# A state space layer on one core: the quarter turns move from TensorE to ScalarE, and TensorE multiplies constants ahead of some waits

## The chip, the cores and the metric

The kernel runs on one core of one Trainium2 chip. Its engines work in parallel and are ordered by semaphores: TensorE (PE, with its weight loads PEld), VectorE (DVE), ScalarE (ACT), GpSimd (POOL) and SyncE (SP), whose queue issues most transfers. The metric is the device time of one launch in microseconds, the median of the runs.

## The reference, cut to what matters

The whole is a stack of layers over 512 tokens of width 1024: an S5 layer, gated feed-forward layers, an attention layer, and then a second block (a Mamba-2 layer and a differential attention layer). The change touches the first layer alone:

```python
def s5_mixer(xn, w_in, lam_re, lam_im, b_re, b_im, c_re, c_im, d_skip, log_dt, w_glu):
    u = (xn @ w_in)                       # 512 x 1024, 64 groups of 16 inputs
    a_bar = exp(lam * dt)                 # complex, 64 states for each group
    b_bar = ((a_bar - 1.0) / lam)[..., None] * b_mat
    s = recurrence(s = a_bar * s + b_bar @ u_t)   # along the sequence
    y = real(s @ c) + d_skip * u
    val, gate = split(gelu(y) @ w_glu)
    return val * sigmoid(gate)
```

The states are complex. The kernel keeps the 64 real parts of a group in partitions 0 to 63 and the 64 imaginary parts in partitions 64 to 127. It takes 8 tokens as one step, so that 64 steps remain, and removes the phase: it multiplies the input of step c by the phase exp(-i c t), runs a real recurrence with the decay alone (one scan instruction), and turns the result back by exp(i c t). A complex product of that kind needs the vector itself and the vector turned by a quarter, (re, im) to (-im, re), which exchanges the two halves of the partitions and changes one sign.

## The kernel before, in words

The S5 layer lies at about 10 to 205 us of the span. Its 64 groups are taken in eight octets, q = 0 to 7. One list, S5_ORDER (s5_order, L90), is walked by every engine's own program (s5_pe, s5_act, s5_dve, s5_pool, s5_sp); each engine does its part of a step and skips the steps in which it has none, strictly in the order of the list. In the loop over q the steps are, in order: `drive q+1`, `scan q`, `inB q+2`, `state q`, then at q = 2 and 3 half of the last input product, `turnB q+2`, `swap q+1`, `inC q+2`, `read q`, `near q+2`, and at some q post steps (the skip term, GELU and the splitting of the result for the next product).

What each does for an octet:

- `inB` and `inC` (combine, L2087): VectorE builds the tables Bp and CA out of powers of a_bar and B or C, three large elementwise instructions each.
- `turnB`: TensorE transposes Bp into PSUM banks 2 and 3 (L2114), ScalarE copies them out to BT (L2122).
- `near`: TensorE makes the short range kernel out of Bp and CA (bank 4, L2132), ScalarE copies it out (ksb, L2143), SP's queue stores it and loads it back as a table Mt.
- `drive`: TensorE multiplies BT by the inputs U (bank 6, L2177). ScalarE makes the sines and cosines s and c of the octet (L2211, L2212, L2215), copies the product out to V (L2218), and starts the angles of the next octet: eight small copies with a scale (angles_act, L2194).
- `swap`: TensorE multiplies V by the constant matrix mturn, a quarter turn (bank 7, L2245).
- `scan`: VectorE forms turned V times s (L2253), V times c (L2256), their sum (L2258), and runs the recurrence (L2263), which writes Ss.
- `state`: TensorE multiplies Ss by the constant matrix turn (bank 0, L2269). VectorE multiplies that by s into H (L2281) and Ss by c in place (L2283; from q = 5, APART, a third instruction adds both, L2285 and L2287). ScalarE makes the decays of the next octet (rho_act, L2225).
- `read`: TensorE waits for H, then multiplies Mt by U and CA by H and by Ss (bank 1; L2297, L2299, L2300, from q = 5 L2297 and L2302). ScalarE copies the result out (Y, L2310), SP's queue stores it.

The scan of q waits until read q-1 is over, since that reads Ss. The weights of the input products are split in two parts by ScalarE (L390) and VectorE (L401) shortly ahead of their product. After the loop the gated output product follows, and then the rest of the network.

Of the kernel before, what the change touches and what calls it, by code (L numbers as in the profile page):

```python
# [8 lines left out]
P = 128  # L9
T = 512  # L10
# [6 lines left out]
NC = 64  # L17
# [24 lines left out]
for _name, _w in PARAMS:  # L42
# [3 lines left out]

CONSTS = [("ones", 128), ("sel", 32), ("spread", 128), ("ident", 128), ("ntri", 128), ("nones", 128),
          ("upper", 128), ("slower", 128), ("nupper", 128), ("low", 128), ("alibi", 512)]
S5_CONSTS = [("turn", 128), ("mturn", 128), ("count", 64)]
CCOL = {}  # L50
_n = 0
for _name, _w in CONSTS:
# [25 lines left out]


def s5_constants():  # L80
    turn = np.zeros((P, P))
    turn[np.arange(64) + 64, np.arange(64)] = -1.0
    turn[np.arange(64), np.arange(64) + 64] = 1.0
    count = np.broadcast_to(np.arange(64.0)[None, :], (P, 64))
    return np.concatenate([turn, -turn, count], axis=1).astype(np.float32)

# [9 lines left out]
def s5_order():  # L98


    posts = {3: "0a 1a", 4: "2a 3a"}
    out = [("dense", 0), ("use", 0), ("dense", 1), ("use", 1), ("load", 0), ("prep", 4),
           ("dense", 2), ("use", 2),
           ("load", 1), ("prep", 5), ("dense", 3), ("use", 3), ("prep", 6), ("dense", 4), ("inB", 0), ("turnB", 0),
           ("use", 4), ("dense", 5), ("prep", 7), ("drive", 0), ("inC", 0), ("near", 0), ("loadbc", 3), ("inB", 1),
           ("use", 5), ("turnB", 1), ("swap", 0), ("inC", 1), ("dense", 6), ("near", 1)]
    for q in range(8):
        if q < 4:
            out.append(("loadbc", q + 4))
        if q < 6:  # L110
            out.append(("load", q + 2))
        if q < 7:
            out.append(("drive", q + 1))
        if q == 6:
            out.append(("splithigh", 0))
        out.append(("scan", q))
        if q < 6:
            out.append(("inB", q + 2))
        if q == 0:
            out.append(("use", 6))  # L120
        if q == 6:
# [12 lines left out]
        if q < 6:
            out.append(("turnB", q + 2))
        if q < 7:
            out.append(("swap", q + 1))
        if q == 4:
            out += [("postb", 0), ("postb", 1)]
        if q < 6:  # L140
            out.append(("inC", q + 2))
        if q == 3:
            out.append(("use", 7))
        if q == 7:
            out.append(("glu", 0))
# [1819 lines left out]
W = NQ  # L1965
# [2 lines left out]
GS = [slice(q * W, (q + 1) * W) for q in range(8)]  # L1968
LOW, UP = slice(0, 64), slice(64, 128)
APART = 5  # L1970


def flat(x):
# [130 lines left out]
    dve.e.tensor_tensor(by_lag(dst, n), by_lag(dst, n), by_lag(K.Bs, n), ALU.add).then_inc(K.S["mat"], 1)  # L2104


def turn_b_pe(K, pe, q):
    pe.wait_ge("mat", 2 * q + 1)
    pe.wait_ge("ld", 16)
    pe.wait_ge("ld5", 16)  # L2110
    for j in range(2):
        take(pe, 2 + j, ("BT", 2 * q + j + 1))
        for i in range(4):
            mm = pe.e.transpose(K.bank[2 + j][:, i * P:(i + 1) * P], K.Bp[:, 4 * j + i, :], K.con("ident"))  # L2114
        mm.then_inc(K.S["BTp"], 1)
# [9 lines left out]

def near_pe(K, pe, q):

    pe.wait_ge("mat", 2 * q + 2)
    take(pe, 4, ("ksb", 2 * q + 2))
    for g in range(8):  # L2130
        j, i = g // 4, g % 4
        mm = pe.e.matmul(K.bank[4][32 * j:32 * j + 16, i * P:(i + 1) * P], K.Bp[:, g, 0:16], K.CA[q % 3][:, g, 0:P],  # L2132
                         start=(i == 0), stop=True, skip_group_check=True)
    mm.then_inc(K.S["Kp"], 1)
# [35 lines left out]


def drive_pe(K, pe, q):
    take(pe, 6, ("V", q + 1))
    pe.wait_ge("BT", 2 * q + 2)
    pe.wait_ge(f"ul{q % 3}", 128 * (q // 3 + 1))
    for i in range(8):
        mm = pe.e.matmul(K.bank[6][:, i * NC:(i + 1) * NC], K.BT[q % 2][:, i, :], K.U[q % 3][:, i, :], start=(i == 0),  # L2177
                         stop=True, skip_group_check=True)
    mm.then_inc(K.S["Vp"], 1)

# [26 lines left out]
def drive_act(K, act, q):  # L2207
    c, s = K.rot[q % 2][:, 0], K.rot[q % 2][:, 1]
    act.wait_ge("trig", q + 1)
    act.other("sin")  # L2210
    act.e.activation(s, K.rsc[:, :, :], ACT.Sin, scale=-6.283185).then_inc(K.S["rot"], 1)  # L2211
    act.e.activation(c, K.rsc[:, :, :], ACT.Abs, scale=6.283185).then_inc(K.S["rot"], 1)  # L2212
    act.wait_ge("rot", 4 * q + 2)
    act.wait_ge("prep", 2)
    act.e.activation(c, c, ACT.Sin, scale=-1.0, bias=K.quarter[:, :]).then_inc(K.S["rot"], 1)  # L2215
    act.wait_ge("Vp", q + 1)
    act.wait_ge("vr", q - 1)
    act.e.activation(flat(K.V[q % 2]), K.bank[6][:, :], ACT.Copy).then_inc(K.S["V"], 1)  # L2218


def rho_act(K, act, q):
# [17 lines left out]
                               op1=ALU.subtract).then_inc(K.S["trig"], 1)  # L2239


def swap_pe(K, pe, q):
    take(pe, 7, ("vr0", q + 1))
    pe.wait_ge("V", q + 1)
    pe.e.matmul(K.bank[7][:, :], K.five("mturn"), flat(K.V[q % 2]), start=True, stop=True).then_inc(K.S["turned"], 1)  # L2245


def scan_dve(K, dve, q):
    c, s, V, e = K.rot[q % 2][:, 0], K.rot[q % 2][:, 1], K.V[q % 2], dve.e
    dve.wait_ge("turned", 2 * q + 1)  # L2250
    dve.wait_ge("rot", 4 * q + 1)
    dve.wait_ge("S", q)
    e.tensor_tensor(K.vr[:, :, :], K.bank[7][:, :].rearrange("p (g c) -> p g c", g=W), s, ALU.mult).then_inc(  # L2253
        K.S["vr0"], 1)
    dve.wait_ge("rot", 4 * q + 3)
    own(K, dve, "dve", e.tensor_tensor(V[:, :, :], V[:, :, :], c, ALU.mult))  # L2256
    dve.wait_ge("vr0", q + 1)
    e.tensor_tensor(K.vr[:, :, :], K.vr[:, :, :], V[:, :, :], ALU.add).then_inc(K.S["vr"], 1)  # L2258
    dve.wait_ge("rot", 4 * q + 4)
    dve.wait_ge("vr", q + 1)  # L2260
    dve.wait_ge("H", q)
    dve.wait_ge("Yp", min(q, APART))
    e.tensor_tensor_scan(flat(K.Ss), flat(K.rho), flat(K.vr), 0.0, ALU.mult, ALU.add).then_inc(K.S["S"], 1)  # L2263


def state_pe(K, pe, q):
    take(pe, 0, ("H0", q + 1))
    pe.wait_ge("S", q + 1)
    pe.e.matmul(K.bank[0][:, :], K.five("turn"), flat(K.Ss), start=True, stop=True).then_inc(K.S["turned"], 1)  # L2269


def state_dve(K, dve, q):


    c, s, S, H, e, n = K.rot[q % 2][:, 0], K.rot[q % 2][:, 1], K.Ss, K.H, dve.e, NC - 1
    b = K.bank[0][:, :].rearrange("p (g c) -> p g c", g=W)
    dve.wait_ge("Yp", q)
    if q == APART:
        e.memset(H[:, :, 0:1], 0.0).then_inc(K.S["dve"], dve.up())
    dve.wait_ge("turned", 2 * q + 2)  # L2280
    e.tensor_tensor(H[:, :, 1:NC], b[:, :, 0:n], s[:, :, 0:n], ALU.mult).then_inc(K.S["H0"], 1)  # L2281
    if q < APART:
        e.tensor_tensor(S[:, :, 0:n], S[:, :, 0:n], c[:, :, 0:n], ALU.mult).then_inc(K.S["H"], 1)  # L2283
        return
    own(K, dve, "dve", e.tensor_tensor(S[:, :, 0:n], S[:, :, 0:n], c[:, :, 0:n], ALU.mult))  # L2285
    dve.wait_ge("H0", q + 1)
    e.tensor_tensor(H[:, :, 1:NC], H[:, :, 1:NC], S[:, :, 0:n], ALU.add).then_inc(K.S["H"], 1)  # L2287


def read_pe(K, pe, q):  # L2290
    take(pe, 1, ("Y", q + 1))
    pe.wait_ge("H0", q + 1)
    pe.wait_ge("H", q + 1)
    pe.wait_ge(f"mt{q % 2}", 128 * (q // 2 + 1))
# [103 lines left out]
def s5_pe(K, pe):  # L2398
# [6 lines left out]
    for what, q in S5_ORDER:  # L2405
# [3 lines left out]
            product_half(K, pe, "a_w_in", 7, FIRST[7], x, ("us", 8), q)  # L2409
        elif what == "drive":  # L2410
            drive_pe(K, pe, q)
        elif what == "swap":
            swap_pe(K, pe, q)
        elif what == "state":
            state_pe(K, pe, q)
        elif what == "read":
            read_pe(K, pe, q)
        elif what == "turnB":
# [21 lines left out]
def s5_act(K, act):  # L2440
# [13 lines left out]
    for what, q in S5_ORDER:  # L2454
# [6 lines left out]
        elif what == "drive":  # L2461
# [2 lines left out]
                rho_act(K, act, 0)  # L2464
            if q < 7:
                angles_act(K, act, q + 1)
        elif what == "state" and q < 7:
            rho_act(K, act, q + 1)
        elif what == "read":
            read_act(K, act, q)  # L2470
        elif what == "turnB":
# [714 lines left out]
```

## Time and profile before

| what | value |
|---|---|
| median of 3 runs | 2039.47 us (2038.74 to 2039.65) |
| profiled execution, its own time | 2048.49 us |
| its span | 2046.7 us |
| PE busy | 1969.8 us, 96% |
| DVE busy | 1380.8 us, 67% |
| ACT busy | 865.7 us, 42% |
| granted TensorE clock, mean | 0.987 |

The span is the time from the first to the last instruction of the profiled execution, and that execution took some 9 us longer than the median of the runs. The granted clock is a share of TensorE's full speed: 1.00 is 2.4 GHz, 0.50 is 1.2 GHz.

### The profile page before, as it was taken

What the parts mean: (1) busy time and instruction counts of PE and PEld (TensorE: products, weight loads), DVE (VectorE), ACT (ScalarE), POOL (GpSimd) and SP (SyncE); (2) the same over time, 40 slices, a digit from 0 to 9 for tenths busy, and PEclk for the clock granted to TensorE, in tenths of its full rate; (3) what the DMA queues carried; (4) which work ended last, traced back from release to release, by engine and by line L of the source; (5) the groups of instructions that cost most, each with busy time, mean ns of one, the idle gap of its engine ahead of it and who ended that gap; (6) DMA issues with size and microseconds to landing.
All of it is one profiled execution on the core that took longest, in us unless ns stands there. A gap on an engine that the chain in (4) does not pass through costs nothing.

```text
span 2046.7 us, 24942 instructions
## 1 busy us (share of the span) xinstructions
PE 1969.8 (96%) x9404; PEld 1566.5 (77%) x9404; DVE 1380.8 (67%) x2046; ACT 865.7 (42%) x1342; POOL 254.1 (12%) x231
## 2 busy tenths in 40 slices
PE   7899999999999999999999999899999998999997
PEld 5687888888888776788888888687777776886665
DVE  7986467536654448747645654888888888437986
ACT  4554343222233338733222233444444444236773
POOL 3030100000001000010000001224333331000002
PEclk9898999999999999999999999999999999999998
DMA  7454323232233220022233323221222223322112
GB/s 224 107 126 129 114 82 105 80 123 85 89 95 106 91 92 21 1 93 92 82 105 104 103 79 100 73 67 53 83 73 83 78 63 93 103 73 74 35 32 78
DMA packets 79623, 178.33 MB, mean 87 GB/s; under 512 B 17680, under 2 KB 31248, under 8 KB 79504
## 3 DMA queue, kind: packets, MB, share of 16 engines
q1 hardware_dynamic: 75792, 169.92, 26.8%
q0 software_dynamic: 3424, 6.23, 1.3%
q8 instruction: 75, 1.23, 0.2%
q10 hardware_dynamic: 288, 0.59, 0.1%
q14 instruction: 44, 0.36, 0.1%
HBM read 169.43 MB, written 7.27 MB: 86 GB/s over the span
## 4 chain that ended last, share of the span: by engine, by line
PE 71%; DVE 18%; ACT 5%; issue 5%; DMA 0%; POOL 0%; DVEq 0%; POOLq 0%; ACTq 0%
PE psum L430 16%; PE psum L433 16%; PE psum L431 16%; DVE wl L401 2%; PE psum L471 2%; PE psum L472 2%; PE psum L474 2%; PE psum L855 1%; PE psum L856 1%; PE psum L857 1%; ACT wh L390 1%; PE psum L452 1%; DVE mE L1654 1%; PE psum L455 1%; DVE mE L1673 1%
## 5 line engine op out<-in xcount | busy, mean ns | idle before, releaser
L401 DVE TENSOR_TENSOR wl<-raw,wh 128x1024 fp32r<-128x1024 f32 (+3 forms) x337 | 391.7, 1164 | 330.8 <-ACT wh L390 330.3
L430 PE MATMUL psum<-xh,wh 128*128 128x512 f32 x1368 | 542.6, 397 | 1.2 <-DVE mbc L1531 0.9
L433 PE MATMUL psum<-xh,wl 128*128 128x512 f32 x1368 | 534.0, 390 | 1.3 <-DVE wl L401 1.3
L431 PE MATMUL psum<-xl,wh 128*128 128x512 f32 x1368 | 533.5, 390 | 0.0
L390 ACT ACTIVATE wh<-raw 128x1024 fp32r<-128x1024 f32 (+3 forms) x337 | 315.4, 938 | 275.3 <-PE psum L433 167.7
L430 PEld LDWEIGHTS psum<-xh,wh 128*128 128x128 f32 x1368 | 257.4, 188 | 62.2 <-issue 3.4
L433 PEld LDWEIGHTS psum<-xh,wl 128*128 128x128 f32 x1368 | 257.3, 188 | 57.2 <-DVE wl L401 2.9
L431 PEld LDWEIGHTS psum<-xl,wh 128*128 128x128 f32 x1368 | 257.5, 188 | 55.4 <-issue 2.9
L578 POOL TENSOR_TENSOR rs<-rs,sq 128x512 f32<-128x512 f32 x41 | 54.3, 1323 | 1092.3 <-ACT sq L563 1092.2
L430 PE MATMUL psum<-fh,wh 128*128 128x512 f32 x352 | 136.9, 389 | 0.0
L431 PE MATMUL psum<-fl,wh 128*128 128x512 f32 x352 | 136.9, 389 | 0.0
L433 PE MATMUL psum<-fh,wl 128*128 128x512 f32 x352 | 136.9, 389 | 0.0
L675 DVE TENSOR_TENSOR h<-h,psum 128x512 f32<-128x512 f32 x88 | 60.1, 683 | 70.0 <-PE psum L433 67.6
L471 PE MATMUL psum<-xh,wh 128*128 128x512 f32 x160 | 67.1, 420 | 13.1 <-ACT wh L390 10.8
L431 PEld LDWEIGHTS psum<-fl,wh 128*128 128x128 f32 x352 | 66.1, 188 | 13.8
L433 PEld LDWEIGHTS psum<-fh,wl 128*128 128x128 f32 x352 | 66.1, 188 | 13.8
L430 PEld LDWEIGHTS psum<-fh,wh 128*128 128x128 f32 x352 | 66.1, 188 | 13.7
L541 ACT ACTIVATE xh<-h,par 128x512 fp32r<-128x512 f32 x64 | 44.1, 716 | 64.0 <-DVE h L675 55.3
L1663 ACT ACTIVATE mE<-psum 128x384 f32<-128x384 f32 x32 | 15.7, 491 | 117.2 <-DVE mE L1654 117.2
L474 PE MATMUL psum<-xh,wl 128*128 128x512 f32 x160 | 63.2, 395 | 0.0
L472 PE MATMUL psum<-xl,wh 128*128 128x512 f32 x160 | 63.1, 395 | 0.0
L727 ACT ACTIVATE ny<-ny 128x512 f32<-128x512 f32 x22 | 13.9, 632 | 110.3 <-DVE ny L764 110.3
(498 smaller groups left out, 3362.5 us busy)
## 6 DMA issues: line engine op xcount, KB each, us to landing
raw<-d_w SPq DMA_DIRECT2D x224, 512.0 KB, 3.5
raw<-d_w SPq DMA_DIRECT2D x32, 384.0 KB, 3.1
raw<-d_w SPq DMA_DIRECT2D x48, 256.0 KB, 2.6
raw<-d_w SPq DMA_DIRECT2D x32, 320.0 KB, 2.9
Mt<-d_kd SPq DMA_DIRECT2D x64, 64.0 KB, 2.4
bc<-d_bc SPq DMA_DIRECT2D x8, 256.0 KB, 3.4
d_ud<-ust SPq DMA_DIRECT2D x8, 256.0 KB, 3.1
U<-d_ud POOLq DMA_DIRECT2D x64, 32.0 KB, 3.0
```

The source lines that it names most:

```text
L390: act.e.activation(K.wh[n % NH][:, 0:COLS[n]], K.raw[n % RAW][:, 0:COLS[n]], ACT.Copy).then_inc(K.S["hi"], 1)
L401: dve.e.tensor_tensor(K.wl[n % NH][:, 0:COLS[n]], K.raw[n % RAW][:, 0:COLS[n]], K.wh[n % NH][:, 0:COLS[n]].bitcast(F32), ALU.subtract).the ...
L430: pe.e.matmul(b[:, :], WH[:, o:o + P], XH, start=(k == k0), stop=False)
L431: pe.e.matmul(b[:, :], WH[:, o:o + P], XL, start=False, stop=False)
L433: mm = pe.e.matmul(b[:, :], WL[:, o:o + P], XH, start=False, stop=(k == k1 - 1))
L452: pe.e.matmul(b[:, :], WH[:, o:o + P], XH, start=(k == 0), stop=False)
L471: pe.e.matmul(b[:, :], WH[:, o:o + P], XH, start=(k == 0), stop=False)
L472: pe.e.matmul(b[:, :], WH[:, o:o + P], XL, start=False, stop=False)
L474: mm = pe.e.matmul(b[:, :], WL[:, o:o + P], XH, start=False, stop=(k == 7))
L541: act.e.activation(K.xh[:, k, :], K.h[:, k, :], ACT.Copy, scale=K.par(gain, k)).then_inc(K.S["xh"], 1)
L578: pool.e.tensor_tensor(K.acc[:, :], K.acc[:, :], K.sq[k % 2][:, :], ALU.add).then_inc(K.S["acc"], 1)
L675: dve.e.tensor_tensor(K.h[:, m, :], K.h[:, m, :], K.bank[bank][:, :], ALU.add).then_inc(K.S[signal], 1)
```

## The change

The two constant matrices go, and with them the steps `swap` and the TensorE part of `state`. ScalarE makes the quarter turn instead, as two copies of 64 partitions each, the lower half into the upper and the upper into the lower, one of them with the scale -1: once out of the drive's PSUM bank in place of the copy to V (so V now holds the turned vector), once out of Ss into V (state_act). VectorE reads the vector that isn't turned straight from the drive's bank, which alternates between 6 and 7. TensorE gets 23 matmuls of the identity by 512 columns of constants, whose result nobody reads; they are issued ahead of the wait of turnB, near or read of the octets that the three tuples name.

```diff
-S5_CONSTS = [("turn", 128), ("mturn", 128), ("count", 64)]
+S5_CONSTS = [("count", 64)]
@@ s5_order: the steps ("swap", q) are gone
+BUSY_TURN = (5, 3, 3, 3, 0, 0, 3, 2)
+BUSY_NEAR = (0, 0, 2, 0, 0, 0, 0, 0)
+BUSY_READ = (0, 0, 0, 0, 0, 0, 1, 1)
+def busy_pe(K, pe, bank, n):
+    first = CCOL["spread"][0]
+    for _ in range(n):
+        pe.e.matmul(K.bank[bank][:, :], K.con("ident"), K.all_con[:, first:first + T], start=True, stop=True)
 def turn_b_pe(K, pe, q):
-    pe.wait_ge("mat", 2 * q + 1)
     ...
         take(pe, 2 + j, ("BT", 2 * q + j + 1))
+        if j == 0:
+            busy_pe(K, pe, 2, BUSY_TURN[q])
+            pe.wait_ge("mat", 2 * q + 1)
 def near_pe(K, pe, q):
+    take(pe, 4, ("ksb", 2 * q + 2))
+    busy_pe(K, pe, 4, BUSY_NEAR[q])
     pe.wait_ge("mat", 2 * q + 2)
-    take(pe, 4, ("ksb", 2 * q + 2))
 def drive_pe(K, pe, q):
-    take(pe, 6, ("V", q + 1))
+    bank = 6 + q % 2
+    take(pe, bank, ("vr0", 2 * q + 1))
 def drive_act(K, act, q):
     ...
-    act.wait_ge("vr", q - 1)
-    act.e.activation(flat(K.V[q % 2]), K.bank[6][:, :], ACT.Copy).then_inc(K.S["V"], 1)
+    act.wait_ge("H0", q - 1)
+    V, b = flat(K.V[q % 2]), K.bank[6 + q % 2]
+    act.e.activation(V[LOW, :], b[UP, :], ACT.Copy).then_inc(K.S["V"], 1)
+    act.e.activation(V[UP, :], b[LOW, :], ACT.Copy, scale=-1.0).then_inc(K.S["V"], 1)
+def state_act(K, act, q):
+    act.wait_ge("S", q + 1)
+    S, turned = flat(K.Ss), flat(K.V[q % 2])
+    act.e.activation(turned[LOW, :], S[UP, :], ACT.Copy, scale=-1.0).then_inc(K.S["turned"], 1)
+    act.e.activation(turned[UP, :], S[LOW, :], ACT.Copy).then_inc(K.S["turned"], 1)
-def swap_pe(K, pe, q): ...
-def state_pe(K, pe, q): ...
 def scan_dve(K, dve, q):
-    dve.wait_ge("turned", 2 * q + 1)
+    dve.wait_ge("Vp", q + 1)
+    dve.wait_ge("rot", 4 * q + 3)
     dve.wait_ge("S", q)
     # first product: the drive's bank times c, then V (turned) times s, then the sum
 def state_dve(K, dve, q):
     dve.wait_ge("turned", 2 * q + 2)
-    e.tensor_tensor(H[:, :, 1:NC], b[:, :, 0:n], s[:, :, 0:n], ALU.mult).then_inc(K.S["H0"], 1)
+    e.tensor_tensor(H[:, :, 1:NC], K.V[q % 2][:, :, 0:n], s[:, :, 0:n], ALU.mult).then_inc(K.S["H0"], 1)
 def read_pe(K, pe, q):
     take(pe, 1, ("Y", q + 1))
+    busy_pe(K, pe, 1, BUSY_READ[q])
 def s5_act(K, act):
         elif what == "drive":
             drive_act(K, act, q)
             ...
             if q < 7:
                 angles_act(K, act, q + 1)
-        elif what == "state" and q < 7:
-            rho_act(K, act, q + 1)
+        elif what == "state":
+            state_act(K, act, q)
+            if q < 7:
+                rho_act(K, act, q + 1)
```

## Rows read from the trace of the kernel before

**Rows 1.** Stages with each engine's busy time, granted clock (PEclk), DMA share.
```profile
93.60:97.40 3.80, 1.42 (x10) 1.13 (x10) 3.77 (x6) 3.38 (x12) 0.00 (x0) 1.00 0.37 80
97.40:111.00 13.60, 13.60 (x65) 12.14 (x64) 8.30 (x9) 1.75 (x4) 1.59 (x4) 0.50 0.18 43
...
169.10:172.50 3.40, 2.53 (x23) 2.56 (x23) 3.28 (x5) 0.19 (x1) 0.00 (x0) 1.00 0.52 137
172.50:189.50 17.00, 16.35 (x58) 13.66 (x58) 8.47 (x13) 7.19 (x11) 2.67 (x5) 0.50 0.51 148
```

**Rows 2.** PE's waits, 40 to 190 us: total, times, longest.
```profile
PE psum L2114 <- DVE Bp L2104: 11.4, 5, 4.4
```

**Rows 3.** VectorE in order of time, octets 3 and 4: start, length.
```profile
138.20 1.22 DVE L2263 TENSOR_TENSOR_SCAN xs<-rho,sq 128x512 f32<-128x512 f32 x1 [0.74 <-PE psum L2300]
142.85 0.68 DVE L2281 TENSOR_TENSOR H<-psum,rot 128x504 f32<-128x504 f32 x1
...
145.36 1.35 DVE L2096 TENSOR_TENSOR Bs<-pw,bc 128x1152 f32<-128x1152 f32 x1
149.29 0.69 DVE L2238 SCALAR_TENSOR_TENSOR sq<-rot,sq 128x512 f32<-128x512 f32 x1
151.99 1.23 DVE L2263 TENSOR_TENSOR_SCAN xs<-rho,sq 128x512 f32<-128x512 f32 x1
```

**Rows 4.** ScalarE in order of time, the same turn of the loop.
```profile
139.59 1.20 ACT L2143 ACTIVATE ksb<-psum 16x512 f32<-16x512 f32 x2 [0.89 <-PE psum L2132]
...
142.61 0.60 ACT L2218 ACTIVATE V<-psum 128x512 f32<-128x512 f32 x1
143.11 2.01 ACT L2194 ACTIVATE sq<-five,tau 128x64 f32<-128x64 f32 x8
145.02 0.61 ACT L2225 ACTIVATE rho<-s5small 128x504 f32<-128x504 f32 x1
```

**Rows 5.** TensorE in order of time, the same turn and the read ahead.
```profile
132.60 0.33 PE L2297 MATMUL psum<-U,Mt 128*128 128x64 f32 x2
...
138.00 1.50 PE L2132 MATMUL psum<-CA,Bp 128*16 128x128 f32 x16
139.43 2.00 PE L2177 MATMUL psum<-U,BT 128*128 128x64 f32 x16
...
142.99 1.09 PE L2114 MATMUL psum<-con,Bp 128*128 128x128 f32 x8 [0.66 <-DVE Bp L2104]
143.93 1.02 PE L2245 MATMUL psum<-V,five 128*128 128x512 f32 x2
144.79 0.33 PE L2297 MATMUL psum<-U,Mt 128*128 128x64 f32 x2
```

**Rows 6.** TensorE in order of time, octet 1, where the clock falls.
```profile
96.17 1.09 PE L2114 MATMUL psum<-con,Bp 128*128 128x128 f32 x8 [2.38 <-DVE Bp L2104]
97.10 1.62 PE L2245 MATMUL psum<-V,five 128*128 128x512 f32 x2
98.51 0.53 PE L2297 MATMUL psum<-U,Mt 128*128 128x64 f32 x2
...
108.78 2.56 PE L2132 MATMUL psum<-CA,Bp 128*16 128x128 f32 x16
```

**Rows 7.** VectorE, first and last product into H (octets 0 and 7).
```profile
79.95 0.67 DVE L2281 TENSOR_TENSOR H<-psum,rot 128x504 f32<-128x504 f32 x1
...
176.66 0.68 DVE L2281 TENSOR_TENSOR H<-psum,rot 128x504 f32<-128x504 f32 x1 [2.43 <-PE psum L2269]
```

**Rows 8.** ScalarE and TensorE near the loop's end, and ScalarE's first instruction.
```profile
175.39 1.28 ACT L2351 ACT_TABLE_LOAD   x1
178.53 0.63 ACT L2354 ACTIVATE xh<-py 128x512 fp32r<-128x512 f32 x1
185.72 0.77 PE L2385 MATMUL psum<-xl,wh 128*128 128x512 f32 x1
5.50 1.28 ACT L2993 ACT_TABLE_LOAD   x1 [5.50 <-DMA five<-d_five]
```

More of the change, by code:

```diff
@@ L80, in s5_constants @@
 def s5_constants():
[L81 to L85, printed above, removed]
+    return np.broadcast_to(np.arange(64.0)[None, :], (P, 64)).astype(np.float32)
 def pieces(k0, k1):
@@ L105, in s5_order @@
            ("use", 4), ("dense", 5), ("prep", 7), ("drive", 0), ("inC", 0), ("near", 0), ("loadbc", 3), ("inB", 1),
-           ("use", 5), ("turnB", 1), ("swap", 0), ("inC", 1), ("dense", 6), ("near", 1)]
+           ("use", 5), ("turnB", 1), ("inC", 1), ("dense", 6), ("near", 1)]
     for q in range(8):
@@ L135, in s5_order @@
             out.append(("turnB", q + 2))
-        if q < 7:
-            out.append(("swap", q + 1))
         if q == 4:
@@ L2176, in drive_pe @@
     for i in range(8):
-        mm = pe.e.matmul(K.bank[6][:, i * NC:(i + 1) * NC], K.BT[q % 2][:, i, :], K.U[q % 3][:, i, :], start=(i == 0),
+        mm = pe.e.matmul(K.bank[bank][:, i * NC:(i + 1) * NC], K.BT[q % 2][:, i, :], K.U[q % 3][:, i, :], start=(i == 0),
                          stop=True, skip_group_check=True)
@@ L2239, in drive_dve @@
                                op1=ALU.subtract).then_inc(K.S["trig"], 1)
[L2242 to L2245, printed above, removed]
 def scan_dve(K, dve, q):
     c, s, V, e = K.rot[q % 2][:, 0], K.rot[q % 2][:, 1], K.V[q % 2], dve.e
-    dve.wait_ge("turned", 2 * q + 1)
-    dve.wait_ge("rot", 4 * q + 1)
[L2252 to L2257, printed above, removed]
+    dve.wait_ge("Vp", q + 1)
+    dve.wait_ge("rot", 4 * q + 3)
+    dve.wait_ge("S", q)
+    e.tensor_tensor(K.vr[:, :, :], K.bank[6 + q % 2][:, :].rearrange("p (g c) -> p g c", g=W), c,
+                    ALU.mult).then_inc(K.S["vr0"], 1)
+    dve.wait_ge("V", 2 * q + 2)
+    dve.wait_ge("rot", 4 * q + 1)
+    e.tensor_tensor(V[:, :, :], V[:, :, :], s, ALU.mult).then_inc(K.S["vr0"], 1)
+    dve.wait_ge("vr0", 2 * q + 2)
     e.tensor_tensor(K.vr[:, :, :], K.vr[:, :, :], V[:, :, :], ALU.add).then_inc(K.S["vr"], 1)
@@ L2263, in scan_dve @@
     e.tensor_tensor_scan(flat(K.Ss), flat(K.rho), flat(K.vr), 0.0, ALU.mult, ALU.add).then_inc(K.S["S"], 1)
[L2266 to L2269, printed above, removed]
 def state_dve(K, dve, q):
     c, s, S, H, e, n = K.rot[q % 2][:, 0], K.rot[q % 2][:, 1], K.Ss, K.H, dve.e, NC - 1
-    b = K.bank[0][:, :].rearrange("p (g c) -> p g c", g=W)
     dve.wait_ge("Yp", q)
@@ L2411, in s5_pe @@
             drive_pe(K, pe, q)
[L2412 to L2415, printed above, removed]
         elif what == "read":
```

## The prediction

> **What bounds the kernel now.** The page first: TensorE is busy for nearly the whole span, so the end of the kernel moves by what TensorE loses or wins anywhere. The stages then show where it loses in the S5 layer: at 97.4 to 111.0 and at 172.5 to 189.5 us the granted clock is 0.50, that is 1.2 GHz, and what it does there takes twice as long [rows 1]. Third the waits: the longest of TensorE's are those of the transposes for VectorE's table Bp, 11.4 us in five pieces [rows 2]. Last the three engines in order of time over one turn of the loop at the full clock (octets 3 and 4), which shows how they hang together.
>
> VectorE in one turn: scan and inB 142.85 - 138.20 = 4.65, the two products of state 0.68 each (1.2 until the next can start), inC 149.29 - 145.36 = 3.93, and the rounding and three products 151.99 - 149.29 = 2.70: 12.5 us [rows 3]. TensorE in one turn: read 138.00 - 132.60 = 5.40, near 1.50, drive 2.00, transposes and the two quarter turns about 2.8, and at q = 2 and 3 half a product, 2.7 more: 11.7 or 14.4 [rows 5]. So VectorE sets the pace, except at q = 2 and 3 and where TensorE is at the low clock. ScalarE is not late: it reaches its place for the step state (L2225) at 145.02, and nobody needs it there; H is made from 142.85 on, with the turn that TensorE did [rows 3, 4].
>
> **The change, part by part.**
>
> 1. The turns leave TensorE: 16 matmuls of about 0.9 us (143.93 to 144.79 [rows 5]), 14 us of its work, more at the low clock. Its turn of the loop falls to 9.9 or 12.6 us. That is worth time only where nothing else is later, and part 2 is.
>
> 2. The turns come to ScalarE. A half copy has 512 elements in each partition like the whole one, and a copy of 16 partitions by 512 takes 0.60 like one of 128 [rows 4], so I take 0.60 for a half and 0.50 + 0.60 = 1.1 for a pair; the bounds are 0.6 (half the time each) and 1.3 (no overlap). V costs 0.5 more, state a pair more: 1.6 in each turn. ScalarE's sum allows for it; its order does not. The list has drive q+1 ahead of state q, and ScalarE is strict: copy of ksb, sine, modulus, cosine, V, eight angles, and only then the turn of Ss. Ahead of them stands the wait for near q+1, which TensorE does after read q-1, which waits for H of q-1. That closes a loop through three engines. From the start of near to the place of state 145.02 - 138.00 = 7.02; second half of V 0.50; the pair 1.1; the two products into H and Ss 1.3; hand-over to TensorE 0.2; read 5.40: 15.5 us a turn, against VectorE's 12.5 [rows 3 to 5]. VectorE then stands 3 us in each turn ahead of L2281, and queued behind it on VectorE are inC (which near q+2 waits for) and the next scan.
>
>  Added up from H of octet 0 to H of octet 7, which are 176.66 - 79.95 = 96.7 apart now [rows 7]: 0 to 1: 15.5 and the two multiplications ahead of near 2, about 0.85 each, which have no idle time left to fill, 17.2. 1 to 4: 3 x 15.5 = 46.5. 4 to 5: the sine table's load on top, 1.3 by the other load's 1.28 [rows 8]: 16.8. 5 to 6: the read is a third shorter (16 products for 24, 3.6), H has a third product (0.7), the angles (145.02 - 143.11 = 1.9 [rows 4]) are gone, a weight split of about 1.0 comes in front: 13.4. 6 to 7: products into H 2.0, hand-over 0.2, read 3.6, copy Y 0.6, then the GELU pair, 178.53 + 0.63 - 175.39 = 3.8 [rows 8], ahead of the turn, 1.1: 11.3. Sum 105.2, so H of octet 7 is 8.5 later. H of octet 0 I leave where it is: turnB's and near's earlier ends give up to 1.0 there, ScalarE's order takes up to 1.3.
>
>  At the full clock the last read is 5.8 after that H, against 185.72 - 176.66 = 9.1 at the low one now [rows 7, 8]: 3.3 back. What follows runs at 0.50 until 189.5 [rows 1]; 1.9 more comes back if it does not. 8.5 - 3.3 - 1.9 = 3.3 us slower with the clock up throughout.
>
> 3. The clock. It fell at 97.4 after TensorE had been idle for 2.38 us and then did transposes and part of a turn (1.42 of 3.80 us busy), and at 172.5 after 0.9 idle and part of a read (2.53 of 3.40 busy); and it stayed at 0.50 through the whole read, 98.51 to 108.78, and rose only with near behind it [rows 1, 6]. Now the gap ahead of a read: from the start of near to H ready 7.02 + 0.5 + 1.1 + 1.3 + 0.2 = 10.1, less TensorE's work, near 1.4, drive 1.9, three multiplications 2.6 (or half a product, 2.7) and the transposes 0.9: 3.3 idle, right behind transposes and right ahead of a read. That is more idle than where it fell, in every turn, and the tuples put something in front of this very wait only at q = 6 and 7, one product where four microseconds and more are idle. A read at the low clock costs 10.27 - 5.40 = 4.87, a short one two thirds of each, 3.25, near 2.56 - 1.50 = 1.06 [rows 5, 6]. If it falls ahead of all: 5 x 4.87 + 5 x 1.06 + 2 x 3.25 + 1.06 + 3.25, and the 1.9 not given back: 42.4. Where it falls in the middle of a read, as at 172.5, or not at all, less is lost; I take three quarters, 32.
>
> 4. The 19 multiplications ahead of transposes: they stand ahead of waits of 11.4 us in all [rows 2], and the removed turns leave gaps there too. The five and three at octets 0 and 1 keep the clock up where VectorE waits little for TensorE: gain 0 to 1.0, inside the allowance for H of octet 0. Later ones are hidden by the loop of part 2: 0.
>
> 5. The constants: the table `five` shrinks from 512 to 256 columns. ScalarE's first instruction waits for it at 5.50 [rows 8]; the x that the second needs comes in beside it. Gain 0 to 1.2; I take 0.5.
>
>  Sum: 3.3 + 32 - 0.5 = 35 us, so 2048.5 + 35 = 2083.5 for the profiled execution's own time. That lies 9.0 above the median of the runs, and the difference is carried over: 2039.5 + 35 = 2074.
>
>  A page bears on part 3. The clock fell 1.2 us after the transposes at 96.17 had begun, and they did not hold it [rows 6]. The Trainium skill, page "TensorE: Matmul & The Clock Gate", Part 4: PE-mode transpose, states that transposes do not count as work for the clock as matmuls do. By that rule the stretch ahead of each read that does nothing for the clock is 3.3 + 0.9 = 4.2 us, and the case of part 3 holds for every turn (the full 42); if they counted in full, it would be 3.3, and the case without falls gains some chance.
>
> **The rivals.**
>
> A, my forecast: the order on ScalarE sets the turn, and the clock falls ahead of most reads. 2074; its own range 2060 to 2086.
>
> B, the same order, but the clock holds. For it: an idle time of 0.66 us at 142.99 passed without a fall [rows 5], 0.9 us was enough only in front of a read [rows 1], and three multiplications now stand close ahead of each gap. Against it: the gap is 3.3 us, longer than either of those before which it fell, and a read follows. 3.3 - 0.5: 2042, and up to 2055 if two or three reads are slow.
>
> C, faster: ScalarE's turn is in time. The mechanism is VectorE's pace of 12.5 us, with TensorE's turns gone and the clock up. The price: seven intervals at VectorE's pace with the extras of today (14.0 + 38 + 13.8 + 11.0 + 6.5 = 83.4 against 96.7), 3.3 for the last read and 1.9 behind it: 18.5 faster, 2021. It decides from the point where ScalarE needs, from the start of near to the end of the turn, no more than 12.5 - 5.4 - 1.5 = 5.6 us; by the rows it needs 7.02 + 0.5 + 1.1 = 8.6, by the lower bound of the copies 7.9. For it speaks only that ScalarE is idle for much of the loop.
>
> D, the multiplications don't hold the clock ahead of transposes at all and cost where the wait is shorter than they are: 23 x 0.9 = 21 us at most, of which 11 and more is covered; it comes on top of A and leads to its upper end, 2086.
>
> **How the numbers follow.** A with D 0.63, B 0.23, C 0.14. A difference under 0.2% (4 us: 2035.4 to 2043.5) can't be told from none. Faster: C and a little of B's start, 0.15. Same: the half of B with hardly a slow read, 0.11. Slower: 0.74. The range goes from 2034, which leaves C out, to 2086, the sum with every fall (3.3 + 42.4 - 0.5 = 45).
>
> **What would show it.** In the changed kernel's trace: VectorE idle for some 3 us ahead of the product into H in each octet, released by ScalarE's copy of the half; ScalarE's pair directly behind the eight angles; 15 to 21 us from H to H; TensorE idle ahead of L2297's successor and not ahead of the transposes; clock 0.50 in most reads; no matmul out of V or Ss. My forecast is wrong if the idle time before H is under 1 us (then C), or if it is 3 us and the clock is 1.00 in the reads (then B).

## The result and the profile after

The changed kernel takes 2093.19 us (median of 4 runs, 2091.70 to 2094.13), the kernel before 2039.56 in the same session (4 runs, 2038.74 to 2040.13). The ratio is 1.0254, with a 95% interval of 1.0229 to 1.0279: slower by 53.6 us. The forecast was 2074, with 2086 as its upper end: the direction is right, the size is not.

The profiled execution's own time is 2092.76 and its span 2090.9. The page of the kernel after, busy time of each engine and the row of the granted clock in 40 slices:

```profile
PE 2000.3 (96%) x9418; PEld 1590.7 (76%) x9418; DVE 1381.9 (66%) x2046; ACT 882.0 (42%) x1366; POOL 254.1 (12%) x231
...
PEclk9877799999999999999999999999999999999999
```

The low digits stand at the start and nowhere else. How much of the loss lies there is read from one event, the first copy of h behind the S5 layer. Before (the execution that the forecast read), its start and length:

```profile
205.51 0.66 DVE L2551 COPY h<-nv 128x512 f32<-128x512 f32 x1
```

And after, with the products into H of the octets 0, 3 and 7 (they answer to [rows 3, 7]):

```profile
80.67 0.68 DVE L2287 TENSOR_TENSOR H<-V,rot 128x504 f32<-128x504 f32 x1 [1.67 <-ACT V L2236]
...
148.31 0.68 DVE L2287 TENSOR_TENSOR H<-V,rot 128x504 f32<-128x504 f32 x1 [5.19 <-ACT V L2236]
...
220.49 0.68 DVE L2287 TENSOR_TENSOR H<-V,rot 128x504 f32<-128x504 f32 x1 [8.44 <-ACT V L2236]
...
249.57 0.68 DVE L2556 COPY h<-nv 128x512 f32<-128x512 f32 x1
```

From that copy to the end of the span it is 2046.7 - 205.51 = 1841.2 before and 2090.9 - 249.57 = 1841.3 after. In the profiles of all kernels here it is 1840.8 to 1842.8. So the whole difference lies in the S5 layer, and the time of this copy measures it to within 2 us. From H of octet 0 to H of octet 7 it is 139.8 now, 96.7 before.

VectorE's waits after, 40 to 240 us (total, times, longest), and under them TensorE's that answer to [rows 2]:

```profile
DVE H L2287 <- ACT V L2236: 42.9, 8, 8.4
...
PE psum L2304 <- DVE xs L2289: 10.1, 4, 3.8
PE psum L2120 <- DVE Bp L2101: 1.7, 2, 0.9
```

VectorE stands for 42.9 us in eight pieces ahead of the product into H, and each time it is ScalarE's second half copy that lets it go. The wait of the transposes for Bp has shrunk from 11.4 to 1.7; the idle time has moved behind them, to the read.

The chain that ended last, in the turn of octet 3 (start, length, what; most issue rows and the middle of the read left out). It is the loop that the forecast described:

```profile
137.95 2.67 PE psum L2139 x15
...
140.70 0.59 ACT ksb L2150
...
141.31 0.59 ACT ksb L2150
141.90 0.52 ACT rot L2219
142.41 0.53 ACT rot L2220
...
143.72 0.59 ACT V L2227
...
144.34 0.59 ACT V L2228
...
144.95 2.02 ACT sq L2202 x8
...
147.00 0.03 ACT V L2235
147.03 0.62 issue
147.65 0.64 ACT V L2236
...
148.31 0.68 DVE H L2287
149.00 0.60 DVE xs L2289
149.60 0.24 issue
149.84 0.41 PE psum L2304 x2
...
157.81 0.43 PE psum L2307 x2
158.24 1.80 PE psum L2139 x10
```

Near, ksb, sines, V, eight angles, the turn, the two products, the read, near again: 20.3 us. From ksb to the second half of V ScalarE works for octet 4, and the angles are for a later one still; the turn of state 3 (L2235, L2236), which stands behind them, needs none of it. In the read the length of one entry doubles from 0.22 to 0.43 at 152.26. Two stretches of the same turn (start:end length; busy time and instructions of TensorE, its weight loads, VectorE, ScalarE, GpSimd; granted clock, DMA share, GB/s), the gap ahead of the read and the read, which answer to [rows 1]:

```profile
145.00:149.80 4.80, 1.86 (x13) 1.41 (x11) 1.49 (x3) 4.72 (x14) 0.00 (x0) 1.00 0.67 171
149.80:158.20 8.40, 8.36 (x49) 8.27 (x50) 6.77 (x8) 0.71 (x2) 1.06 (x2) 0.64 0.25 71
```

### The profile page after: what moved, and what is told of

Its sections match the earlier page's. It is cut to its first block, busy times and chain, and to the rows that moved or that the text cites. A ratio compares the mean times of both kernels' runs of the same rounds, so it can differ in the third digit from the quotient of the medians.

```text
span 2090.9 us, 24976 instructions
## 1 busy us (share of the span) xinstructions
PE 2000.3 (96%) x9418; PEld 1590.7 (76%) x9418; DVE 1381.9 (66%) x2046; ACT 882.0 (42%) x1366; POOL 254.1 (12%) x231
## 3 DMA queue, kind: packets, MB, share of 16 engines
q8 instruction: 75, 1.23, 0.2%
## 4 chain that ended last, share of the span: by engine, by line
PE 70%; DVE 17%; ACT 7%; issue 5%; DMA 0%; POOL 0%; POOLq 0%; DVEq 0%; ACTq 0%; SPq 0%
PE psum L424 16%; PE psum L427 16%; PE psum L425 16%; DVE wl L395 2%; PE psum L465 2%; PE psum L468 2%; PE psum L466 2%; PE psum L849 1%; PE psum L851 1%; PE psum L850 1%; PE psum L2304 1%; ACT wh L384 1%; DVE mE L1648 1%; PE psum L446 1%; DVE mE L1667 1%
## 5 line engine op out<-in xcount | busy, mean ns | idle before, releaser
L465 PE MATMUL psum<-xh,wh 128*128 128x512 f32 x160 | 67.2, 420 | 13.0 <-ACT wh L384 10.7
L2304 PE MATMUL psum<-U,Mt 128*128 128x64 f32 x128 | 36.7, 385 | 27.8 <-issue 10.4
```

The costliest lines, as they stand in the source:

```text
L465: pe.e.matmul(b[:, :], WH[:, o:o + P], XH, start=(k == 0), stop=False)
L2304: pe.e.matmul(o, K.Mt[q % 2][:, i, :], K.U[q % 3][:, i, :], start=(i == 0), stop=False, skip_group_check=True)
```

## The experiments

They are compared by the median, and where it is given by the time of the first copy of h, by the granted clock of 40 to 200 us and by VectorE's wait ahead of H. "q" is the octet. Each ratio is against runs of the kernel before in the same session. Their medians were 2038.85 (session of e0 to e3), 2043.70 (e5, e6, e8, e9) and 2040.54 (e4, e7, e10), so medians of different sessions compare only to a few microseconds.

### e0: the kernel before once more

No edit.

> The kernel before, unchanged, profiled again. The profiled execution of the prediction took 2048.5 us, 9.0 more than the median of the runs. Theory (that execution was an unlucky one: its clock was at 0.50 for longer in the S5 layer than is usual): the new profile's own time is near 2040, and the S5 layer has fewer or shorter stretches at 0.50 than 97.4 to 111.0 and 172.5 to 189.5; its last read ends some 8 us earlier than 185.7. Rival (a profiled execution of this kernel always costs about 9 us more, anywhere): about 2048 again, with the same stretches.

Measured: 2039.94 (8 runs), ratio 1.0003 [0.9984, 1.0023]. Its profile is another one than that of the forecast. The kernel before as the forecast read it:

```profile
40.00:200.00 160.00, 143.61 (x857) 118.68 (x856) 129.28 (x151) 82.21 (x167) 37.56 (x72) 0.88 0.50 130
```

The same kernel in this run, with the stretch that answers to the last of [rows 1] and the first copy of h:

```profile
172.50:189.50 17.00, 15.69 (x85) 13.63 (x86) 8.60 (x13) 7.73 (x13) 1.07 (x2) 1.00 0.71 231
40.00:200.00 160.00, 141.86 (x899) 116.23 (x898) 135.39 (x158) 88.73 (x175) 38.21 (x73) 0.96 0.52 135
...
195.48 0.66 DVE L2551 COPY h<-nv 128x512 f32<-128x512 f32 x1
```

The copy comes at 195.48 and not at 205.51, and the span is 2036.8 and not 2046.7. The execution that the forecast read lost 10 us more, all within the S5 layer and with more time at the low clock (0.88 against 0.96); the median of the runs in the table before belongs to the other kind. Of the 25 runs of before beside e5, twelve lie at 2038.0 to 2040.6, eight at 2048.1 to 2050.4, and five between. So the kernel before has both kinds in it, and the rival (a profiled execution always costs 9 us more) is refuted.

### e1: the turn ahead of the next drive

```diff
         elif what == "drive":
+            if q:
+                state_act(K, act, q - 1)
             drive_act(K, act, q)
...
-        elif what == "state":
-            state_act(K, act, q)
+        elif what == "scan" and q == 7:
+            state_act(K, act, q)
```

and one wait for V more ahead of VectorE's first product, which would otherwise read V too early.

> The changed kernel, but ScalarE turns Ss ahead of drive q+1 (behind the copy of ksb) instead of behind the eight angles, and at q = 7 ahead of the GELU pair; VectorE's first product waits for both halves of V. Theory (the order on ScalarE makes the loss, by the idle time of VectorE ahead of H and by the low clock that follows from TensorE's gap): VectorE's wait ahead of the product into H, 42.9 us in eight pieces, falls under 5; H to H 12.5 to 14 us; 2018 to 2030 us. Rival 1 (the extra copies load ScalarE, wherever they stand): the wait moves to the products of the scan, H to H 15 us and more, 2045 to 2070. Rival 2 (the multiplications of constants cost time themselves): 2035 to 2050.

Measured: 2045.54 (10 runs), ratio 1.0022 [1.0007, 1.0037]; first copy of h 200.63. VectorE's wait ahead of H, 75 to 175 us:

```profile
DVE H L2288 <- ACT V L2236: 3.9, 2, 3.0
```

42.9 us of wait have become 3.9, and 47.7 of the 53.6 us are gone by this one move in a list. Rival 1 (the load) would have put the wait in front of the scan's products; what stands there is 1.3 us in one piece. H to H is 12.6 to 14.6 us from octet 1 to 6. The expected 2018 to 2030 was missed all the same: the clock is 1.00 to 150 us and falls then.

```profile
40.00:150.00 110.00, 102.58 (x677) 81.39 (x676) 103.97 (x118) 74.64 (x149) 33.81 (x65) 1.00 0.54 133
150.00:190.00 40.00, 37.07 (x168) 31.52 (x169) 24.27 (x32) 22.19 (x41) 3.25 (x6) 0.66 0.47 118
```

What stands ahead of that fall are two gaps of TensorE, of 1.15 and 1.02 us, around eight transposes (start, length, and in brackets the idle time before and its releaser):

```profile
148.54 1.09 PE L2120 MATMUL psum<-con,Bp 128*128 128x128 f32 x8 [1.15 <-DVE Bp L2101]
...
150.66 0.62 PE L2305 MATMUL psum<-U,Mt 128*128 128x64 f32 x2 [1.02 <-DVE H L2294]
```

### e2: the late order, with products ahead of each read

```diff
-BUSY_READ = (0, 0, 0, 0, 0, 0, 1, 1)
+BUSY_READ = (3, 4, 3, 3, 3, 5, 6, 5)
```

> The changed kernel with BUSY_READ = (3, 4, 3, 3, 3, 5, 6, 5): TensorE multiplies constants in the gap ahead of every read. ScalarE's order stays. Theory (of the loss, about 10 us are the order's and some 35 the low clock's): clock 1.00 in most reads, VectorE still idle 3 us and more ahead of H, H to H 15.5 to 16, time 2042 to 2055. Rival (the low clock is a by-product, the reads are hidden behind ScalarE anyway): under 5 us faster than the changed kernel, 2088 and more.

Measured: 2064.30 (4 runs), ratio 1.0105 [1.0076, 1.0133]; first copy of h 222.09. Waits of VectorE and the stages:

```profile
DVE H L2287 <- ACT V L2236: 32.1, 8, 6.2
...
40.00:200.00 160.00, 153.04 (x845) 113.55 (x843) 121.74 (x141) 93.78 (x183) 37.37 (x71) 0.93 0.45 114
```

The granted clock of 40 to 200 rises from 0.78 to 0.93 and 29 us come back, with the order on ScalarE as in the change. Where read and near ran at the full clock, H to H is 17.8 (octets 0 to 1) and 16.1 (1 to 2), against the 17.2 and 15.5 of the forecast. The expected 2042 to 2055 is missed. Two stretches were still at the low clock (118.8 to 135.8 and 190.0 to 196.5), and at octet 3 the products themselves were late: they began at 136.63, and the read behind them at 139.21, 2.4 us behind VectorE's last product for it (136.81). VectorE's wait falls from 42.9 to 32.1: that part of it came with the clock, since a slow read makes the next near late. The rival's under 5 us is refuted.

### e3: the change without its products

```diff
-BUSY_TURN = (5, 3, 3, 3, 0, 0, 3, 2)
-BUSY_NEAR = (0, 0, 2, 0, 0, 0, 0, 0)
-BUSY_READ = (0, 0, 0, 0, 0, 0, 1, 1)
+BUSY_TURN = BUSY_NEAR = BUSY_READ = (0,) * 8
```

> The changed kernel with all three tuples zero. Theory (the 23 products keep nothing up behind octet 1, since the clock falls ahead of the reads all the same, and two of them ahead of near 2 and three ahead of turnB 3 and 6 run at the low clock): within 5 us of the changed kernel's 2093, on either side. Rival (they hold the clock for drive and transposes): 2100 to 2115.

Measured: 2100.19 (4 runs), ratio 1.0285 [1.0259, 1.0311]; clock of 40 to 200 us 0.70, VectorE's wait ahead of H 48.0 in eight. The products don't cost 11 to 21 us as rival D had it; they gain 7.0 by the medians. That is 2 more than the theory allowed and at the lower end of the rival (2100 to 2115), by which they hold the clock for some of the work: it is 0.70 without them and 0.78 with them.

### e5: the turn only ahead of the angles

```diff
             drive_act(K, act, q)
+            if q:
+                state_act(K, act, q - 1)
...
-            state_act(K, act, q)
+            if q == 7:
+                state_act(K, act, q)
```

Each turn now stands behind ksb, sines and V of the next octet, but ahead of its eight angles.

> The changed kernel, but ScalarE turns Ss between the copies of V and the eight angles, 1.9 us earlier in each turn of the loop than in the changed kernel and 4 us later than in e1. Theory (what counts is how late ScalarE's turn is; its load is the same in all three): VectorE's wait ahead of H falls from 42.9 us by 1.9 x 7 or more, TensorE's gap ahead of the reads by as much, and with it some reads stay at 1.00; 2050 to 2070, between e1 and the changed kernel. Rival (only the load counts): as the changed kernel, 2090.

Measured: 2072.62 (4 runs), ratio 1.0133 [1.0104, 1.0161]; first copy of h 230.05; VectorE's wait 29.2 us in seven pieces. It lies between the late order (2093.2) and the early one (2045.5), 20.6 from the first and 27.1 from the second, and 2.6 over the 2070 that was expected at most.

### e6: the kernel before with the products alone

```diff
+BUSY_TURN = (5, 3, 3, 3, 0, 0, 3, 2)
+BUSY_NEAR = (0, 0, 2, 0, 0, 0, 0, 0)
+BUSY_READ = (0, 0, 0, 0, 0, 0, 1, 1)
```

with busy_pe at the same three places; both quarter turns stay TensorE's.

> The kernel before with TensorE's own quarter turns, and the 23 products of constants at the same places as in the changed kernel. It does the second part of the change alone. Theory (the products are harmless and hold the clock at octets 0, 1 and 3, where VectorE or TensorE gain a little): 2030 to 2038. Rival (they cost where the wait is shorter than they are, octets 2, 6 and 7): 2040 to 2050.

Measured: 2038.30 (10 runs), ratio 0.9973 [0.9958, 0.9989]; first copy of h 192.50. The same row as above:

```profile
40.00:200.00 160.00, 155.93 (x952) 122.52 (x951) 136.90 (x160) 88.93 (x176) 37.11 (x72) 1.00 0.53 138
```

TensorE is busy for 14.1 us more than in e0, and the copy of h comes 3.0 us earlier all the same: the products lie in its idle time, and in this execution the clock doesn't fall between 40 and 200 us. That is the part of the change that gains, 0.27% with an interval of 0.11 to 0.42%. The median is 0.3 above the expected 2030 to 2038. Much of the gain is that the long executions are gone: the ten runs lie at 2035.3 to 2039.3, while 13 of the 25 runs of before beside them took 2043.7 or more. Against the kernel before's 2039.56 of the first session it would be 0.06%.

### e4: the early order without the products

As e1, with the three tuples at zero.

> e1's order (ScalarE turns Ss behind the copy of ksb) with all three tuples zero: with e1, e3 and the changed kernel it makes a square of order and products. Theory (the gaps in this order are 1 to 3 us, so that products in them decide over the clock): 2048 to 2062, with stretches at 0.50 behind octets 0, 1 and 3 and at the end. Rival (the products matter only with the late turn): 2040 to 2047, as e1.

Measured: 2059.49 (5 runs), ratio 1.0076 [1.0044, 1.0107]; clock of 40 to 200 us 0.78. With e3, e1 and the change it makes a square (medians, us):

```
               with products   without   products are worth
late order        2093.2        2100.2          7.0
early order       2045.5        2059.5         14.0
order is worth      47.7          40.7
```

The order is worth 41 to 48 us with and without the products, and the expected 2048 to 2062 came. The products are worth 7 and 14 by the medians; that they are worth more in the early order is likely, not shown. The runs of e4 lie in two groups (2051.7 and 2052.3, and 2059.5 to 2060.2), its profile is one of the first, and the corners come from three sessions. A reason would be that under the late order the long gap stands ahead of the read, where the tuples put nothing before q = 6.

The clock of 40 to 200 us is 0.78 in this profile and in that of the change, and yet they are 41 us apart (2051.7 and 2092.8): here the S5 layer is through at 208.8, there it is at octet 6 by then. So the low clock alone doesn't make the loss.

### e7: straight half copies in place of crossed ones

```diff
-    act.e.activation(V[LOW, :], b[UP, :], ACT.Copy).then_inc(K.S["V"], 1)
-    act.e.activation(V[UP, :], b[LOW, :], ACT.Copy, scale=-1.0).then_inc(K.S["V"], 1)
+    act.e.activation(V[LOW, :], b[LOW, :], ACT.Copy).then_inc(K.S["V"], 1)
+    act.e.activation(V[UP, :], b[UP, :], ACT.Copy, scale=-1.0).then_inc(K.S["V"], 1)
```

> The changed kernel, but the two half copies out of the drive's bank go to the same partitions instead of the other half (V holds the vector with one half's sign changed, not the turned one, so the output is another). In the changed kernel a crossed half took 0.59 us and the next instruction began 0.61 behind its start, where the whole copy of before took 0.60 and the next began 0.50 behind. Theory (crossing costs the overlap): the straight halves begin 0.50 apart. Rival (any copy of 64 partitions loses the overlap): 0.61 apart. The time should be within 5 us of the changed kernel's.

Measured: 2096.44, one run, within the 5 us. ScalarE in the straight kernel (start, length):

```profile
76.30 0.59 ACT L2227 ACTIVATE V<-psum 64x512 f32<-64x512 f32 x1
76.92 0.59 ACT L2228 ACTIVATE V<-psum 64x512 f32<-64x512 f32 x1
77.54 2.03 ACT L2202 ACTIVATE sq<-five,tau 128x64 f32<-128x64 f32 x8
```

The halves start 0.62 apart, straight as they are, and the angles 0.62 behind the second; behind the whole copy of before they start 0.50 behind [rows 4]. The theory that crossing costs the overlap is wrong; the rival holds, that each copy of 64 partitions does without it. Why, stays open.

### e8: the early order, with the products put where its gaps are

As e1, with

```diff
-BUSY_TURN = (5, 3, 3, 3, 0, 0, 3, 2)
-BUSY_READ = (0, 0, 0, 0, 0, 0, 1, 1)
+BUSY_TURN = (5, 3, 3, 3, 0, 0, 3, 3)
+BUSY_READ = (1, 0, 0, 0, 0, 1, 3, 3)
```

> e1 (ScalarE turns Ss behind the copy of ksb) with other numbers of products: BUSY_TURN (5, 3, 3, 3, 0, 0, 3, 3), BUSY_READ (1, 0, 0, 0, 0, 1, 3, 3). In e1 the clock was 1.00 up to 151 us and then 0.50 for 9 and for 17 us, behind gaps of 1.15, 1.02 and 1.65 us ahead of the transposes and reads of octets 5 to 7. Theory (those two stretches are what e1 still loses, some 12 us): 2028 to 2035, clock 1.00 up to 200. Rival (the stretches come from the phase at which the clock is looked at, or the products cost what they save): 2038 to 2046, as e1.

Measured: 2041.02 (10 runs), ratio 0.9983 [0.9965, 1.0001]; first copy of h 198.00. Of e1's two stretches at the low clock one is gone, and the other has shrunk to some 10 us:

```profile
150.00:190.00 40.00, 37.57 (x197) 30.00 (x196) 25.12 (x34) 22.87 (x42) 3.26 (x6) 0.87 0.49 123
```

The expected 2028 to 2035 is missed, and the time is in the rival's 2038 to 2046. From H of octet 6 to H of octet 7 it is 10.7 here and 7.4 in e6, and the longest wait of VectorE there is 2.8 us, for ScalarE's half copy: at the end of the loop the turn is late even in this order.

### e9 and e10: only the turn of V on ScalarE

e9 is the change with the turn of state on TensorE as before (matrix and bank as before); V stays two half copies. e10 adds one product where e9's clock fell.

```diff
-            state_act(K, act, q)
...
+        elif what == "state":
+            state_pe(K, pe, q)
```

```diff
-BUSY_READ = (0, 0, 0, 0, 0, 0, 1, 1)
+BUSY_READ = (0, 0, 0, 0, 0, 1, 1, 1)
```

> The changed kernel with one of its two turns undone: TensorE turns Ss again (matrix turn, bank 0), ScalarE makes the turned V in two half copies, and the 23 products stay. VectorE's first product waits for both halves of V, as in e1. Theory (the turn of Ss on ScalarE makes the whole loss, the turn of V costs 0.6 us of ScalarE that nobody waits for): H to H 12.5 to 14 us as in e1, 2025 to 2040. Rival (half of the loss is V's): 2060 and more.

> e9 (TensorE turns Ss, ScalarE makes V in two half copies) with one product more, BUSY_READ (0, 0, 0, 0, 0, 1, 1, 1). In e9 the only stretch at 0.50 was 152 to 163 us, behind a gap of 1.0 us ahead of read 5. Theory: the clock stays at 1.00 through the loop, H to H 14 and 11 us at octets 4 to 6 instead of 15.3 and 15.2; 2028 to 2034, faster than both kernels. Rival (another fall comes instead, or e9's was that run's phase): 2036 to 2039 as e9.

Measured: e9 2037.54 (10 runs), ratio 0.9974 [0.9956, 0.9991]; e10 2037.79 (12 runs), ratio 0.9974 [0.9957, 0.9991]. Their stages, e9:

```profile
150.00:190.00 40.00, 36.88 (x197) 29.88 (x197) 24.24 (x33) 17.53 (x28) 3.25 (x6) 0.87 0.55 148
```

and e10:

```profile
150.00:190.00 40.00, 37.30 (x203) 30.08 (x202) 24.88 (x34) 19.25 (x30) 3.26 (x6) 0.91 0.55 152
```

e9 is within the expected 2025 to 2040, and its rival (half of the loss is V's, 2060 and more) is refuted: with the turn of Ss back on TensorE the whole loss of the change is gone, and the turn of V on ScalarE costs nothing that can be seen. H to H is 12.5 to 14.3 up to octet 4, and then 15.3 and 15.2 with the low clock there.

e9's low stretch was 152 to 163; with the product in front of it it is gone, and one at 162 to 169 has come. That is e10's rival, and the expected 2028 to 2034 is missed. e6, e9 and e10 can't be told apart: all three are 0.26 or 0.27% faster than the kernel before of their session, and in all three the turn of state is TensorE's.

## Why the forecast was right, and where it was wrong

**The order on ScalarE (part 2): the mechanism was right.** VectorE waits for the half copy in each octet, over 3.7 us in all but the first, and H to H is 25.2, 22.1, 20.4, 20.8, 17.6, 18.8 and 15.0. e1 takes away little but the place in the list, and the time falls by 47.7 us. e5 takes away the angles alone, and it falls by 20.6. e9 puts the turn of state back on TensorE, and nothing of the loss is left.

The forecast was 2074 and the time is 2093.2. The missing 19.1 us are in two places: 44.2 - 35 = 9.2 in the sum, since in the frame of the profile that it read the span grew by 2090.9 - 2046.7 = 44.2, and 54.1 - 44.2 = 9.9 in the step from there to the median.

**"The difference is carried over": the step that failed.** The sum gave 2083.5 for the profiled execution's own time. The profiled execution of before lay 9.0 above its median, and the forecast took this excess for something that both kernels have: 2074, at most 2086. e0 shows what it was: 10 us that this execution lost at the low clock, in the very stretch that the change alters, and that the median execution doesn't lose. The kernel after loses its clock there in any case, so it has no such excess: its own time, 2092.76, is that of its median. Against e0's span it loses 2090.9 - 2036.8 = 54.1, and the medians differ by 53.6. It is this step that put the result out of the range: the sum with every fall comes to 2039.5 + 45 = 2084.5 by it, and without it the same range would have ended at 2095.

**The sizes of part 2: the step that failed inside the sum.** The intervals from H to H in the forecast's terms (us). The low clock's share is what the read took above 5.47 (a short one above 3.7) and near above 1.50:

```
octets                       0-1   1-2   2-3   3-4   4-5   5-6   6-7    sum
forecast, full clock        17.2  15.5  15.5  15.5  16.8  13.4  11.3  105.2
measured                    25.2  22.1  20.4  20.8  17.6  18.8  15.0  139.8
of it read and near, low     5.5   5.8   4.2   4.1   0.0   4.5   3.3   27.4
left                        19.7  16.2  16.2  16.7  17.6  14.3  11.7  112.4
```

What is left is 7.2 more than forecast. The two products ahead of near 2 cost 3.65 (92.31 to 95.96) and not 1.7, as the read before them had left the clock low: 1.9. A pair of half copies costs 1.3, the upper bound, not 1.1: each takes 0.63 and the next starts 0.65 later, and with the V pair 1.23 passes until the angles start, where whole copies start 0.5 apart [rows 4] and 1.0 was forecast. That is 2.9 over the loop. In octet 4 the copies of V waited 0.56 for the drive, which took 3.68 at the low clock and not 2.00. The rest are pieces of 0.1 to 0.2 us in each turn. e2 says the same without a subtraction: its first two intervals, with read and near at the full clock, are 17.8 and 16.1. Smaller terms were off as well: H of octet 0 comes 0.7 later, and the end of the loop gave back 4.8 (28.85 us from H of octet 7 to the copy of h before, 24.01 in e0, where the clock was up), not 3.3 + 1.9. Against e0 (90.4 us from H to H) the loop loses 112.4 - 90.4 = 22.0 at the full clock by its order, and 32.5 more by the low clock that the order's gaps bring; H of octet 0 is 0.4 earlier, and that makes the 54.1.

The Trainium skill, page "ScalarE: Activation LUTs", section "What ACT_TABLE_LOAD costs", states that ACTIVATEs behind one another overlap by about 93 ns. The whole copies of before agree, 0.60 long and 0.50 apart; the half copies of after (0.59 long, 0.61 apart) and of e7 (0.59 and 0.62) don't, and the measurement decides.

**The clock (part 3): right, with some luck.** The forecast added up 42.4 us for a fall ahead of every read, and then put it: "Where it falls in the middle of a read, as at 172.5, or not at all, less is lost; I take three quarters, 32." No row gave the three quarters. But the reads did what the sentence says. The reads of octets 0, 1, 3, 4 and 5 after, with what stands around them:

```profile
82.04 0.66 PE L2304 MATMUL psum<-U,Mt 128*128 128x64 f32 x2 [2.50 <-DVE H L2287]
...
92.31 3.73 PE L2108 MATMUL psum<-con 128*128 128x512 f32 x4
...
107.41 0.41 PE L2304 MATMUL psum<-U,Mt 128*128 128x64 f32 x2 [3.80 <-DVE xs L2289]
107.97 0.64 PE L2307 MATMUL psum<-xs,CA 128*128 128x63 f32 x2
...
158.17 2.73 PE L2139 MATMUL psum<-CA,Bp 128*16 128x128 f32 x16
160.82 3.68 PE L2185 MATMUL psum<-U,BT 128*128 128x64 f32 x16
164.29 5.23 PE L2108 MATMUL psum<-con 128*128 128x512 f32 x6
...
170.65 0.41 PE L2304 MATMUL psum<-U,Mt 128*128 128x64 f32 x2 [0.25 <-DVE xs L2289]
176.12 1.50 PE L2139 MATMUL psum<-CA,Bp 128*16 128x128 f32 x16
...
188.99 0.66 PE L2304 MATMUL psum<-U,Mt 128*128 128x64 f32 x2 [4.84 <-DVE H L2293]
```

Four reads (octets 0, 5, 6 and 7) are at 1.2 GHz from their start: 0.66 for the first pair, 10.3 us for a whole read and 7.1 for a short one. Octet 1's begins at 2.4 GHz and is at 1.2 after half a microsecond (0.41 becomes 0.64). Those of octets 2 and 3 keep 2.4 GHz for 2.2 to 2.4 us. Only octet 4's goes at 2.4 GHz all through, 5.5 us, and near behind it takes 1.50 and not 2.73; ahead of it the three products, at the low clock themselves, had filled the gap but for 0.25 us. The clock cost 27.4 us in the loop and 29.08 - 24.01 = 5.1 behind it, 32.5 in all, against 32. This split is worked out from rows and not tried one by one. e2 shows the clock's part by itself: with the clock at 0.93 in place of 0.78, 29 us return.

The full 42, a fall ahead of every read, to which the forecast's paragraph on transposes leans, did not come. Whether transposes count for the clock is not tried alone by any run here.

**The rivals.** B (clock holds, 2042) is refuted by the clock of 0.78, and so is C (in time, 2021) by the wait. e1, which brings the turn in time, comes to 2045, not 2021, so C's price was wrong too. It took the full clock for granted, and in e1 that falls behind 150 us (0.66). But e6, with the clock at 1.00, needs 89.0 from H of octet 0 to H of octet 7 and not C's 83.4 (whose pieces add up to 83.3); and C took its gain off the median although a part of it, the 3.3 and 1.9 at the end, was the low clock of the one execution, the same error as above. That TensorE's shorter work leaves more gaps for the clock to fall in is argued from its busy time, 149.1 us in e1 against 155.9 in e6 between 40 and 200, and was not tried alone. D (products as a cost) has the wrong sign, by e3 and e4. The transposes' wait shrank as said in part 4, and the clock did hold through the transposes: eight took 1.03 to 1.09 us in each of the seven octets from 60 to 190 us.

**The constants** (0.5) are too small to be seen in any run here.

## What to carry to other kernels

Each engine here walks its list strictly in order, so a piece of work given to an idle engine is only as early as the last thing ahead of it: ScalarE was busy for 42% of the span, and yet the turn of Ss stood behind some 6 us of work that it didn't need (140.70 to 147.00). Read the place in the list before the load, and close the loop through all engines that wait for one another. The turn of V, which nobody waited for, could move for nothing.

Where a wait hands the idle time to TensorE ahead of short matmuls, price the granted clock too: it was 32 of the 54 us here. Then see whether the profiled execution has that loss in it already; a profile that lies 9 us off the median is to be explained, not carried over.

Products of constants ahead of a wait that is there anyway gained 7 to 14 us by the medians where the clock fell often, and 0.27% (0.11 to 0.42) where it fell seldom; where they ran late or at the low clock they cost time themselves (3.65 us for two). They are worth trying alone, before the work that they are to fill in for is moved.

## What the runs showed of the hardware

- Copies of 64 partitions on ScalarE start 0.61 to 0.65 us apart at 512 elements, crossed or straight, whole ones of 128 partitions 0.50 apart; a half copy takes 0.59 from PSUM and 0.63 from SBUF, and a whole one from PSUM 0.60.
- The granted clock mostly did not come back within a read of small fp32 matmuls (64 columns), though TensorE was busy through all of it: 10.3 us at the low clock from 98.51 in the execution of before that the forecast read, 10.3 from 82.04 in after. But it can. In e0 the read that began at 99.99 ran at the low clock, and from 101.88 on at the full one:

```profile
101.16 0.64 PE L2297 MATMUL psum<-U,Mt 128*128 128x64 f32 x2
...
101.88 0.39 PE L2300 MATMUL psum<-xs,CA 128*128 128x63 f32 x2
```

- Idle times as short as 1.15 and 1.02 us, with eight transposes between them, stood ahead of a fall in e1. Longer ones passed without a fall at the read behind them: 1.31 us in e9 (read at 164.55), 1.52 in e0 (at 173.81). The length of one gap doesn't tell whether the clock falls.
- One and the same kernel was 10 us apart between two executions (spans 2036.8 and 2046.7), with a clock of 40 to 200 us of 0.96 and 0.88. Why the clock falls in one and not in the other was not found, nor why in e10 the fall moved on rather than going away.
